# Host-packed weights and a start from feature-major x in a two-layer float32 decoder trunk

## The reference

```python
h = rmsnorm(x, norm_mix[0])                      # x: 256 x 1024
bg, cg, xv = jnp.split(h @ a_w_in, 3, axis=-1)   # a_w_in: 1024 x 3072
y = (bg * causal_dwconv(cg * xv, a_conv)) @ a_w_out
x = x + y
x = x + conv_ffn(rmsnorm(x, norm_ffn[0]), ...)   # up 1024 x 5632, conv of 3 taps, silu, down 2816 x 1024
k, v = split(rmsnorm(x, kv_norm) @ w_kv)         # shared K and V
# layer 2: q = rmsnorm(x, norm_mix[1]) @ b_w_q, causal attention with ALiBi in 8 heads, @ b_w_o,
# then a second conv_ffn, and the final rmsnorm
```

## Time and profile before

| | |
|---|---|
| Median of 3 runs | 580.14 us (580.02 to 580.18) |
| Span of the profiled execution, first to last instruction | 578.3 us |
| Time around the span (median less span) | 1.8 us |
| TensorE busy | 569.7 us (99%) |
| VectorE, ScalarE, GpSimd busy | 422.9, 317.9, 22.8 us |
| DMA | 107.03 MB, mean 185 GB/s |

### The profile page before, as it was taken

How to read it: one execution, slowest core, us unless ns; L and a number is a source line. 1 busy time by engine, 2 the same in 40 slices (tenths; PEclk the granted TensorE clock), 3 DMA queues, 4 the chain that set the end, 5 groups by cost and what they waited for, 6 DMA issues and landing times.

```text
span 578.3 us, 8025 instructions
## 1 busy us (share of the span) xinstructions
PE 569.7 (99%) x3064; PEld 493.2 (85%) x3064; DVE 422.9 (73%) x516; ACT 317.9 (55%) x387; POOL 22.8 (4%) x26
## 2 busy tenths in 40 slices
PE   8999999999999999999999999999999999999996
PEld 7888888888888888888888899888888888888885
DVE  6898886678666666776887688896786666667764
ACT  5744463566645455456455666745656454554543
POOL 1233000000000000000000000000000000000001
PEclk9999999999999999999999999999999999999999
DMA  8996558544666465555655444285455665664002
GB/s 264 348 350 230 198 182 290 175 153 163 203 218 208 164 211 196 174 178 180 219 157 174 180 146 146 82 281 182 147 172 195 216 213 164 205 208 157 0 1 73
DMA packets 81011, 107.03 MB, mean 185 GB/s; under 512 B 1905, under 2 KB 72017, under 8 KB 80977
## 3 DMA queue, kind: packets, MB, share of 16 engines
q1 hardware_dynamic: 80384, 104.84, 54.8%
q10 hardware_dynamic: 592, 1.71, 0.9%
HBM read 105.50 MB, written 1.05 MB: 184 GB/s over the span
## 4 chain that ended last, share of the span: by engine, by line
PE 91%; DVE 2%; ACT 2%; issue 1%; SPq 1%; DMA 1%; POOL 0%; POOLq 0%; DVEq 0%; ACTq 0%
PE pair L1193 37%; PE pair L1201 19%; PE acc L1266 7%; PE acc L1264 7%; PE acc L1262 7%; PE pair L1249 5%; PE pair L1254 3%; PE acc L1176 1%; PE acc L1177 1%; PE acc L1175 1%; DVE wgt L755 1%; DMA raw<-in_a_w_in 1%; PE pair L1276 1%; ACT wgt L432 1%; ACT acc L452 0%
## 5 line engine op out<-in xcount | busy, mean ns | idle before, releaser
L755 DVE TENSOR_TENSOR wgt<-raw,wgt 128x2048 fp32r<-128x2048 f32 x92 | 211.4, 2301 | 53.6 <-ACT wgt L432 53.3
L1193 PE MATMUL pair<-hA,wgt 128*128 128x512 f32 x864 | 205.5, 391 | 0.4 <-DVE wgt L755 0.4
L432 ACT ACTIVATE wgt<-raw 128x2048 fp32r<-128x2048 f32 x93 | 177.4, 1910 | 23.0 <-PE acc L1266 21.6
L1193 PEld LDWEIGHTS pair<-hA,wgt 128*128 128x128 f32 x864 | 160.1, 188 | 32.5 <-issue 0.6
L1201 PEld LDWEIGHTS pair<-hA,wgt 128*128 128x128 f32 x864 | 107.8, 192 | 2.4
L1201 PE MATMUL pair<-hA,wgt 128*128 128x256 f32 x864 | 108.5, 283 | 0.0
L1264 PE MATMUL acc<-wgt,kq_hi 128*128 128x512 f32 x156 | 48.0, 389 | 0.0
L1262 PE MATMUL acc<-wgt,kq_hi 128*128 128x512 f32 x156 | 48.0, 389 | 0.0
L1266 PE MATMUL acc<-wgt,kq_lo 128*128 128x512 f32 x156 | 48.0, 389 | 0.0
L527 ACT ACTIVATE scratch<-scratch 128x512 f32<-128x512 f32 x22 | 13.9, 632 | 59.7 <-DVE scratch L872 59.7
L541 ACT ACTIVATE scratch<-pair 128x512 f32<-128x512 f32 x20 | 11.9, 594 | 58.3 <-PE pair L1201 58.3
(11 more groups left out here) (184 smaller groups left out, 601.4 us busy)
## 6 DMA issues: line engine op xcount, KB each, us to landing
raw<-in_ffn_w_up SPq DMA_DIRECT2D x44, 1024.0 KB, 5.1
raw<-in_ffn_w_down SPq DMA_DIRECT2D x22, 1024.0 KB, 4.9
raw<-in_a_w_in SPq DMA_DIRECT2D x10, 1024.0 KB, 11.8
raw<-in_w_kv SPq DMA_DIRECT2D x8, 1024.0 KB, 5.3
raw<-in_a_w_out SPq DMA_DIRECT2D x4, 1024.0 KB, 5.7
raw<-in_b_w_q SPq DMA_DIRECT2D x4, 1024.0 KB, 5.2
raw<-in_b_w_o SPq DMA_DIRECT2D x4, 1024.0 KB, 5.0
xs<-in_x SPq DMA_DIRECT2D x4, 256.0 KB, 4.3
```

Source lines behind the costliest of these rows:

```text
L432: act.activation(split_slot(s)[0], raw[:, s % RAW, :], ACT.Copy).then_inc(w_hi_ready, 2 if s + 1 in AHEAD else 1)
L755: dve.tensor_tensor(wlo, raw[:, s % RAW, :], whi.bitcast(F32), ALU.subtract).then_inc(w_lo_ready, 2 if s + 1 in AHEAD else 1)
L1193: last = pe.matmul(pair[b][:, e, :].rearrange("p (a n) -> p a n", a=2), whi[:, w], hid[:, :, k, :], start=first and k == 0, stop=not first ...
```

## The change

The host now prepares four arrays: the 98 slots, each laid out as the 128 x 2048 block that goes to `raw` (so that a partition's part of a slot is one run of 8 KB; before, runs of 1 KB from the column slots, of 4 KB from the row slots); x laid out by features, with the columns of `norm_mix[0]` ahead of it; all convolution parameters and two gains in their final layout; and x as it was, which is still loaded, since the squares and the residual need it.

In the kernel the following differs.

- SyncE's loops are written out, one plain transfer for each slot. Its first transfers are: x by features in quarters (260 KB, then 256 KB each), each followed by a quarter of slot 0; slot 1 in halves; the first half of the tokens of x; the first half of slot 2; the other tokens; the second half of slot 2; the parameters (108 KB, one transfer); slots 3 and up.
- ScalarE's `start_hi(k)` scales and rounds one of 8 tiles of 128 features x 256 tokens; VectorE's `start_lo(k)` does scale and subtraction in one instruction. The 16 transposes of x, the `scaled` multiplications, the transposes and copies of parameters are gone.
- VectorE rounds the first quarter of slot 0 (`start_weights`) in ScalarE's place. TensorE warms up with 16 matmuls on a tile that VectorE sets.
- Slot 2 is split and multiplied in halves as well.
- The squares of x come after the splitting of slot 1 on ScalarE, two of them ahead of `mixer_cross(0, 0)`, two between the halves of slot 2. The spreading transposes (line 1446) come after slot 2's "both" part on TensorE.
- VectorE's list changes: `a_whole_sum(0, 0)` now stands between the two halves of slot 1, and `conv_a(0)` stands ahead of `lo(3)`.

The core of the diff:

```diff
-            x_block(0, 0) ... first_quarter(3)
+            for q in range(4):
+                x_columns(q)
+                first_quarter(q)
+            load_half(1, 0, second_landed)
+            load_half(1, 1, landed[1])
+            x_tile(0)
+            load_half(2, 0, third_landed)
+            x_tile(1)
+            load_half(2, 1, landed[2])
+            sp.dma_start(par[:], params).then_inc(par_in, 16)
+            for s in range(3, SLOTS):
+                load(s)
```

```diff
 # ScalarE
-            square(0, 0, 0); start_hi(0, 0); start_hi(1, 0); first_quarter_hi(0); first_quarter_hi(1)
-            start_hi(0, 1); start_hi(1, 1); first_quarter_hi(2); first_quarter_hi(3)
-            second_half_hi(0); square(0, 1, 0); second_half_hi(1); square(0, 0, 1); square(0, 1, 1)
+            for k in range(4):
+                start_hi(k)
+            for q in (1, 2, 3):
+                first_quarter_hi(q)
+                if q < 3:
+                    start_hi(2 * q + 2)
+                    start_hi(2 * q + 3)
+            second_half_hi(0)
+            second_half_hi(1)
+            square(0, 0, 0)
+            square(0, 0, 1)
             mixer_cross(0, 0)
-            hi(2)
+            third_half_hi(0)
+            square(0, 1, 0)
+            square(0, 1, 1)
+            mixer_cross(0, 1)
+            third_half_hi(1)
             act.wait_ge(inv_T, 1)
             act.activation(inv_all, acc[0][0][:, 0:S], ACT.Copy).then_inc(inv_all_ready, 1)
             hi(3)
-            mixer_cross(0, 1)
             hi(4)
```

```diff
 # VectorE
+            def start_lo(k):
+                dve.wait_ge(start_hi_ready, k + 1)
+                dve.scalar_tensor_tensor(out=hA[:, 1, k, :], in0=x_T0[:, k, :], scalar=g_par[:, k:k + 1],
+                                         in1=hA[:, 0, k, :].bitcast(F32), op0=ALU.mult,
+                                         op1=ALU.subtract).then_inc(start_lo_ready, 1)
+            def start_weights():
+                dve.wait_ge(first_landed[0], 16)
+                dve.tensor_copy(split_slot(0)[0][:, 0:COLS // 4], raw[:, 0, 0:COLS // 4]).then_inc(start_w_hi, 1)
...
+            dve.memset(warm_tile[:], 1.0).then_inc(warmed, 1)
+            start_lo(0)
+            start_weights()
+            for k in range(1, 4):
+                start_lo(k)
+            for q in range(1, 4):
+                first_quarter_lo(q)
+                if q < 3:
+                    start_lo(2 * q + 2)
+                    start_lo(2 * q + 3)
             second_half_lo(0)
+            a_whole_sum(0, 0)
+            second_half_lo(1)
             mean_square(0, 0)
+            third_half_lo(0)
             mean_square(0, 1)
             dve.wait_ge(ms_full, 2)
             dve.reciprocal(inv_ms[:], msq[:, :, 1]).then_inc(inv_ready, 1)
-            second_half_lo(1); a_whole_sum(0, 0); lo(2); (parameter copies)
+            a_whole_sum(0, 1)
+            third_half_lo(1)
+            dve.wait_ge(par_in, 16)
+            conv_a(0)
             lo(3)
-            a_whole_sum(0, 1)
-            conv_a(0)
             lo(4)
```

```diff
 # TensorE
+            pe.wait_ge(warmed, 1)
+            for _ in range(16):
+                pe.matmul(pair[1][:, 1, 0:P], warm_tile[:], warm_tile[:], start=True, stop=True)
...
+            first_both(0)
+            for q in range(1, 4):
+                first_both(q)
+                first_narrow(q - 1)
             first_narrow(3).then_inc(slot_done, 1)
             for g in range(2):
                 pe.wait_ge(*((w_hi_ready, 2) if g else (second_hi, 1)))
                 part_both(1, 1, range(4 * g, 4 * g + 4))
+            for g in range(2):
+                pe.wait_ge(*((w_lo_ready, 2) if g else (second_lo, 1)))
+                last = part_narrow(1, 1, range(4 * g, 4 * g + 4))
+            last.then_inc(slot_done, 1)
+            pe.wait_ge(a_sum, a_turn(0, 0))
+            for g in range(2):
+                pe.wait_ge(*((w_hi_ready, 3) if g else (third_hi, 1)))
+                part_both(2, 0, range(4 * g, 4 * g + 4))
+            pe.wait_ge(consts, 1)
             pe.wait_ge(inv_ready, 1)
             (the two spreading transposes, .then_inc(inv_T, 1))
-            (the parameter transposes; narrow part of slot 1)
+            for g in range(2):
+                pe.wait_ge(*((w_lo_ready, 3) if g else (third_lo, 1)))
+                last = part_narrow(2, 0, range(4 * g, 4 * g + 4))
             last.then_inc(slot_done, 1)
+            pe.wait_ge(a_sum, a_turn(0, 1))
+            pe.wait_ge(w_hi_ready, 4)
+            part_both(3, 1, range(KD))
+            wait_slot(3)
+            part_narrow(3, 1, range(KD)).then_inc(slot_done, 1)
-            for i in range(1, KD // 2):
+            for i in range(2, KD // 2):
```

More of the change, by code:

```diff
@@ L33, with slot_order, ffn, build @@
 MASKED = -1e30
-def build(nc, x, norm_mix, norm_ffn, ffn_w_up, ffn_conv, ffn_conv_b, ffn_w_down,
-          a_w_in, a_conv, a_w_out, kv_norm, w_kv, b_w_q, b_w_o, final_norm, out):
+def slot_order(D, F):
+    units = F // 256
+    order = []
+    for i in range(D // 256):
+        order += [("a_w_in", 0, D + 256 * i, False), ("a_w_in", 0, 2 * D + 256 * i, False)]
+    order += [("a_w_in", 0, 256 * i, False) for i in range(D // 256)]
+    order += [("a_w_out", 0, 256 * i, True) for i in range(D // 256)]
+    def ffn(l):
+        pieces = []
+        for j in range(units):
+            pieces += [("ffn_w_up", l, 256 * j, False), ("ffn_w_up", l, F + 256 * j, False)]
+            if j >= 2:
+                pieces.append(("ffn_w_down", l, 256 * (j - 2), True))
+        return pieces + [("ffn_w_down", l, 256 * j, True) for j in (units - 2, units - 1)]
+    order += ffn(0)
+    order += [("w_kv", None, D + 256 * i, False) for i in (0, 1, 3, 2)]
+    for i in range(D // 256):
+        order += [("w_kv", None, 256 * i, False), ("b_w_q", 0, 256 * i, False)]
+    order += [("b_w_o", 0, 256 * i, True) for i in range(D // 256)]
+    return order + ffn(1)
+def build(nc, x, start_x, weights, params, norm_ffn, final_norm, out, F, TAPS):
     _, S, D = x.shape
-    F = ffn_conv.shape[2]
     KD = D // P
     NH = D // P
-    TAPS = ffn_conv.shape[1]
     UNITS = F // (2 * P)
@@ L98, in after @@
         return n if turn is None else n + step * turn
[L100 to L106, removed]
     x_rows = x[0].rearrange("(t p) n -> p t n", p=P)
@@ L300, in _, with load @@
         def _(sp):
-            def load(s, src, turn=None):
+            def load(s):
                 if s >= RAW:
-                    sp.wait_ge(w_lo_ready, after(s - RAW + 1, turn, TURN))
+                    sp.wait_ge(w_lo_ready, s - RAW + 1)
                 if s == RAW:
                     sp.wait_ge(early_lo, 1)
-                sp.dma_start(raw[:, s % RAW, :].rearrange("p (k n) -> p k n", k=src.shape[1]), src).then_inc(landed[s % RAW], 16)
-            def wide(w, c0):
-                return w[:, :, bass.ds(c0, 256)]
@@ L312, in ffn_loads @@
[L312 to L328, removed]
@@ L343, in _ @@
[L343 to L360, removed]
@@ L361, in _ @@
[L361 to L372, removed]
@@ L373, in _, with load_half @@
-            for i in range(KD // 2):
-                load(KQ0 + 2 * i, wide(kv_rows, 256 * i))
-                load(KQ0 + 2 * i + 1, wide(q_rows, 256 * i))
-            for i in range(KD // 2):
-                load(O0 + i, o_rows[:, 2 * i:2 * i + 2, :])
-            ffn_stream(1)
+                sp.dma_start(raw[:, s % RAW, :], weights[s]).then_inc(landed[s % RAW], 16)
+            def load_half(s, g, landing):
+                part = slice(g * COLS // 2, (g + 1) * COLS // 2)
+                sp.dma_start(raw[:, s, part], weights[s, :, part]).then_inc(landing, 16)
@@ new lines, in x_columns, with x_tile @@
+            def x_columns(q):
+                part = slice(KD + 512 * q if q else 0, KD + 512 * (q + 1))
+                sp.dma_start(staged[:, part], start_x[:, part]).then_inc(x_T_in[q], 16)
+            def first_quarter(q):
+                part = slice(q * COLS // 4, (q + 1) * COLS // 4)
+                sp.dma_start(raw[:, 0, part], weights[0, :, part]).then_inc(first_landed[q] if q < 3 else landed[0], 16)
+            def x_tile(t):
+                sp.dma_start(xs[:, t, :], x_rows[:, t, :]).then_inc(x_in[t], 16)
@@ L934, in conv_a @@
                     f = 2 * i + e
-                    tap = [a_par[:, (c + 1) * KD + f:(c + 1) * KD + f + 1] for c in range(TAPS)]
+                    tap = [a_par[:, c * KD + f:c * KD + f + 1] for c in range(TAPS)]
                     dve.tensor_scalar(conv_out[:, f, :], cx[:, e, :], tap[2], None, ALU.mult).then_inc(a_conv_op, 1)
```

231 lines of the change are left out of this document (87 added, 144 removed).

## The result

The changed kernel takes 581.08 us (median of 20 runs, 580.65 to 581.99), the kernel before 579.95 in the same comparison. The ratio is 1.0019 with an interval of 1.0013 to 1.0025: slower by 1.1 us, clear of noise, and not the small gain that I forecast. The ratio leaves out one disturbed run of the kernel before.

What follows compares the result with a forecast made beforehand. TensorE bounds the kernel, so slot 4's start decides: 13.3 + 8.7 + 10.9 = 32.9 against 33.06, 0.2 us sooner, hence 580.14 - 0.2 = 579.9 us. Range 578.5 to 581.5 for 8 in 10.

Steps and rivals of the forecast that it cites:

- What bounds it: TensorE, busy 569.7 of 578.3 us, bounds the kernel; the whole question is when slot 4 starts, 33.06 before.
- Slot 0 done at 12.0: Start of the kernel: slot 0's matmuls, begun at about 5 us, end at 12.0, between 11 and 13.
- TensorE free at 16.6: After slot 0 at 12.0, slot 1 adds 3.64 and half its narrow part 0.96, so TensorE could go on at 16.6.
- X: Landing of the first half of token-major x, which the squares wait for: 13.3 us, between 12.0 and 14.6.
- latest end of 14.6: Latest case for X: first 8 us at 202 GB/s as before, then 395, plus a lag of 1.4 us.
- The walk from X to slot 4: Chain of waits across the engines from X to slot 4's start: 8.7 plus 10.9 us, so slot 4 at 32.9.
- The first part: From X through squares, sum, low half and narrow part to the end of slot 2's both: 8.7 us, ending at 22.0.
- The second part: From slot 2's both through transposes, GpSimd and conv_a(0) to slot 4: 10.9 us, TensorE standing still about 3.0.
- the rival with 3.1 us: GpSimd's first multiplication takes 3.1 us instead of 1.29 even beside an idle VectorE: 581.7 us, chance 0.04.
- No charge for a restart: TensorE's both part of a slot was put at 3.64 us, with nothing added after a wait.
- The second rival: Early transfers stay slow, x comes twice, the squares hold mixer_cross(0, 0): 581.5 us at X = 14.8, chance 0.14.
- The warm-ups: TensorE's 16 warm-up matmuls at the start lie within the wait before the first product, put at about 5 us.

Runs made afterwards that it cites:

- the third experiment: Changed kernel with ScalarE's two squares of the first tokens behind mixer_cross(0, 0) instead of ahead of it: 581.12 us, ratio 1.0017 to the kernel before.
- the first experiment: Changed kernel with the two spreading transposes between the halves of slot 2's both part instead of behind it: 579.3 us, ratio 0.9989 to the kernel before.
- seventh experiments: Changed kernel with the four transfers of x by features issued from ScalarE's queue instead of SyncE's: 581.59 us, ratio 1.0028 to the kernel before.

## Why the prediction was wrong

*What bounds it: right.* The question was when slot 4 starts, and all of the difference is there by the end of its first 16 matmuls.

*Slot 0 done at 12.0, "between 11 and 13": the step that failed.* Its last matmuls start at 12.58 and slot 1 at 13.53, since the second quarter of slot 0 landed at 7.9 and TensorE had 4.8 us of matmuls to do from there. From the start of slot 1 to that of slot 2 TensorE needs 5.57 us without a wait (13.74 to 19.31 in the third experiment), so by this alone slot 2 could not start before 19.1. I had TensorE free at 16.6, and called everything but X off the walk. "Both" of slot 2 ended at 23.2 instead of 22.0, and the chain of after goes there through this landing and TensorE's list.

*X, 13.3: failed too.* I took "13.3: the first 2.1 MB come in runs of 2 KB, between the two, and a little of the lag goes". The square started at 14.52, close to my latest end of 14.6. The first 8 us moved 194 GB/s, no more than before, and the lag did not shrink (at 194 and then 409 GB/s the 3.67 MB were through by 13.2, so it was 1.3 us). The rate I had for later was too low on the other side (409 to 423 against 395). The kernel before held the warning: 202 GB/s over 8 us, with x's 2 KB runs among them; I gave it as the latest case only. In the changed kernel this error cost no more than the 0.2 us that the squares held slot 1's narrow part: with the squares moved away, or x there by 13.8, slot 2 started at 19.31 and 19.47. With slot 0 done at 12.0 it would have cost the same as the other: the two ways were nearly equally long, and either error alone is enough for the miss.

*The walk from X to slot 4: right in its sum, in part by luck.* From the landing of x at 14.5 to slot 4 I had 19.6 us; 14.52 to 33.84 is 19.3. The first part, 14.52 to 23.22, is the 8.7 I had, though it was not the way that decided there, and its terms were off both ways (the two squares took 1.24 us instead of 1.62). The second part, from the end of slot 2's "both" at 23.2 on, took 10.6 against 10.9, most of the difference being the spreading transposes, 0.23 where I had 0.58. It decided, and in it GpSimd's 1.30 us beside an idle VectorE (the rival with 3.1 us is refuted). That the head start is handed back there was forecast, with 3.0 us of standing still against 2.42 measured, and is shown by the first experiment.

*No charge for a restart: failed.* After a wait a group of 16 took 3.94 us instead of 3.64. At slot 4 this is 0.3 of the 1.1 us. The whole account is 1.2 us for the late start, 0.3 less for the second part of the walk, 0.3 for the restart: slot 4's pace is reached at 34.1 instead of the forecast 32.9. Had I put X at 14.5 and changed nothing else, my sum would have given 34.1 as well, with two errors of 0.3 that cancel.

*The second rival* ("the extra megabyte", 581.5 at X = 14.8, chance 0.14) had the slow early transfers and nearly the time. Its reason, that the squares hold everything and every us of X is one of the end, is not what the third and seventh experiments show. *The range* held the time, the sign was missed. Under 230 GB/s in the first 8 us is in every trace here; my row of 395 did not describe the stretch that mattered. The Trainium skill, "DMA: Bandwidth & Descriptors", section Bandwidth, has about 358 GB/s as the bound for transfers from HBM. By that rule X would have been 13.65, also too early. The 409 to 423 GB/s of this single core from 8 us on lie above that bound; the 194 of the first 8 us lie below it, and a bound says nothing on why.

*The warm-ups "lie in that wait": half right.* They lasted to 6.7 us, not 5, and put the first product off by about 1 us, which was covered by the landing at 7.9; yet fewer of them cost 1.4 us. How long the 16 take differs between executions, 5.3 to 6.8 us in the traces.

## What to carry to other kernels

A quicker start is worth only what it brings to the place where the old timing is reached again: follow it there through every engine's list, and look for a small chain (here two transposes, a copy, one GpSimd multiplication) that was moved behind more work. Where two ways to one point are nearly equal, removing one shows nothing, and the forecast needs both. For the first microseconds take the rate of the old kernel's first microseconds, not that of its stream, and add a restart to each wait of TensorE.

## What the runs showed of the hardware

- The first 8 us moved 194 to 227 GB/s in all versions: 202, 197 and 195 in the three with the old start, 194 to 214 with the new start in runs of 2 KB, 226 and 227 with the new start and slots 0 and 1 in runs of 1 KB; a second issuing queue gave 214. From 8 to 30 us the kernel before moved 342 to 349 with runs of 1 KB, the changed kernel 409 to 423 with runs of 2 to 8 KB.
- Early weight transfers completed later when packed into long runs. In the old start the first quarter of slot 0 needed 5.8 us against 4.8 and 4.2. In the new start the second quarter of slot 0 (256 KB) needed 5.5 to 6.4 us with runs of 2 KB (eight traces) and 4.6 and 4.9 with runs of 1 KB. The first quarter of x ahead of them gained nothing by short runs behind it: 3.9 and 4.3 us against 3.0 to 3.3. Run length and place in memory were changed together.
- Matmuls can run at half pace while the granted-clock column reads 1.00: 2.04 instead of 1.17 us for four after little early work, and 7 instead of 12 instructions a us in the warm-ups.
- A wait of TensorE costs some 0.3 us more than its length: 3.91 to 3.96 us for 16 matmuls instead of 3.64.
- A GpSimd multiplication of 1.3 us took 2.62 when VectorE's subtraction of two SBUF tiles had begun before it, and ended 1.15 us after that.
